# Scan stage of a two-layer hybrid mixer: one state step, one scaling and one set of turns moved in the instruction order

## The reference

```python
# latent attention: 4 heads, keys = 128 context + 1024 latent tokens
p = softmax(q @ k.T * scale);  o_mla = p @ v
# GLA, both directions, chunks of 64: gates, scores inside the chunk, state between chunks
q_dec, k_inv = q * exp(g), k * exp(-g)
o = tril(q_dec @ k_inv.T) @ v + q_dec @ s;   s = s * decay + k_end.T @ v
# gated DeltaNet, both directions, chunks of 64, 8 heads
m = strict_tril(k_beta @ k.T * decay)
t_inv = inverse(I + m)                        # triangular, unit diagonal
u, w = t_inv @ (v * beta), t_inv @ (k_beta * exp(g))
v_new = u - w @ s;  o = q_dec @ s + a @ v_new;  s = s * exp(g_last) + k_end.T @ v_new
```

## Time and profile before

| | |
|---|---|
| median of 3 runs | 4552.74 us (4550.39 to 4554.0) |
| profiled execution | 4550.52 us, of which the span is 4548.7 us |
| granted TensorE clock, mean | 0.925 of full speed |
| TensorE matmul / weight load | busy 3934.8 us (87%) / 3081.2 us (68%) |
| VectorE | busy 2176.4 us (48%) |
| ScalarE | busy 970.0 us (21%) |
| GpSimd | busy 1047.1 us (23%) |

### The profile page before, as it was taken

One profiled execution on the slowest core, in us unless ns is written; L12 is line 12 of the kernel. 1 busy time (PEld: TensorE's weight loads), 2 busy tenths in 40 slices (PEclk: granted clock), 3 DMA queues, 4 the chain that ended last, 5 costly groups with the idle time before them and its releaser, 6 DMA issues. The chain is left out here.

```text
span 4548.7 us, 81512 instructions
## 1 busy us (share of the span) xinstructions
PE 3934.8 (87%) x34010; PEld 3081.2 (68%) x34010; DVE 2176.4 (48%) x4932; ACT 970.0 (21%) x1898; POOL 1047.1 (23%) x1092
## 2 busy tenths in 40 slices
PE   4999968888687999999779997788859599999994
PEld 3444546776347999999744444566645399999994
DVE  3335046565455445444453331566646544454444
ACT  1333134444110000000033322444421000000001
POOL 0036034553210000011040440445512101100003
PEclk8999978888888999999989998898879799999997
DMA  7556353331518999999674653243233299999995
GB/s 256 172 192 236 126 126 77 77 73 36 189 63 248 275 278 269 279 278 270 183 233 147 240 192 87 70 99 81 63 117 121 105 271 269 275 278 276 271 279 179
DMA packets 822555, 836.27 MB, mean 184 GB/s; under 512 B 91976, under 2 KB 667528, under 8 KB 816044
## 3 DMA queue, kind: packets, MB, share of 16 engines
q1 hardware_dynamic: 740716, 711.23, 52.3%
q10 hardware_dynamic: 69856, 80.89, 5.3%
q0 software_dynamic: 11616, 38.94, 3.8%
HBM read 698.83 MB, written 132.10 MB: 183 GB/s over the span
## 5 line engine op out<-in xcount | busy, mean ns | idle before, releaser
L2500 PE MATMUL ffn_hb<-ffn_xT,ffn_w 128*128 128x144 f32 x8192 | 1057.4, 288 | 12.9 <-DVE ffn_xT L2613 6.5
L2500 PEld LDWEIGHTS ffn_hb<-ffn_xT,ffn_w 128*128 128x128 f32 x8192 | 1027.9, 191 | 15.7 <-DMA ffn_w<-in_w_e 6.9
L509 PE MATMUL front_acc<-front_w,front_xmT 128*128 128x512 f32 (+2 forms) x2304 | 881.8, 542 | 19.7 <-DVE front_xmT L768 17.4
L509 PEld LDWEIGHTS front_acc<-front_w,front_xmT 128*128 128x128 f32 x2304 | 439.1, 193 | 449.0 <-issue 419.3
L2508 PE MATMUL ffn_acc<-ffn_hT,ffn_w 128*128 128x144 f32 x4096 | 548.5, 287 | 0.0
L2508 PEld LDWEIGHTS ffn_acc<-ffn_hT,ffn_w 128*128 128x128 f32 x4096 | 519.7, 190 | 0.8
L2548 ACT ACTIVATE ffn_en<-ffn_hb 128x144 f32<-128x144 f32 x256 | 74.3, 290 | 1483.7 <-PE ffn_hb L2500 1483.7
L2432 POOL DMA_INDIRECT ffn_xe<-scratch_xhat,ffn_g_idx x34 | 34.5, 1014 | 1376.5 <-DVEq L2602 1376.5
L2647 DVE TENSOR_TENSOR ffn_hT<-ffn_en,ffn_hb 128x144 f32<-128x144 f32 x256 | 77.7, 303 | 529.8 <-ACT ffn_en L2548 528.9
L2224 PE MATMUL mixer_acc<-mixer_wout,mixer_oT 128*128 128x512 f32 x576 | 254.0, 599 | 0.0
L2571 DVE TENSOR_SCALAR_CACHE_REDUCE ffn_junk<-ffn_row,ffn_pair 128x128 f32<-128x128 f32 (+2 forms) x324 | 245.6, 758 | 6.3 <-DVE ffn_yp L2620 4.9
(11 more groups left out here) (322 smaller groups left out, 5195.0 us busy)
## 6 DMA issues: line engine op xcount, KB each, us to landing
ffn_w<-in_w_e SPq DMA_DIRECT2D x768, 512.0 KB, 6.4
x_res<-in_w_mod SPq DMA_DIRECT2D x40, 1024.0 KB, 5.4
x_res<-scratch_proj SPq DMA_DIRECT2D x36, 768.0 KB, 6.1
scratch_proj<-front_out ACTq DMA_DIRECT2D x90, 256.0 KB, 2.2
ffn_row<-scratch_affT SPq DMA_DIRECT2D x36, 576.0 KB, 6.3
front_w<-in_w_in ACTq DMA_DIRECT2D x8, 2048.0 KB, 12.5
scan_qk<-scratch_qkv SPq DMA_DIRECT2D x16, 1024.0 KB, 10.0
scratch_qkv<-x_res SPq DMA_DIRECT2D x18, 768.0 KB, 3.5
```

The lines of the kernel that those rows point to most:

```text
L509: mm = pe.matmul(acc[:, U % 2, 0:size], xmT[:, k, t * P:(t + 1) * P], w[:, n % 2, k, 0:size], start=k == 0, stop=k == KD - 1)
L2500: mm = pe.matmul(hb[:, b, i * CAP:(i + 1) * CAP], w[:, r, k, :], xT[:, s, k, :], start=k == 0, stop=k == KD - 1)
```

## The change

Nothing is added and nothing removed; instructions are placed elsewhere in the engines' programs. L numbers below are those of the kernel before.

```diff
--- before.py
+++ after.py
@@ -1501,32 +1501,32 @@
                     if g > 1:
                         gla_gates(g, h)
                         attend(at + 1)
-                        read_state(k, 2)
                         attend(at + 2)
                         gla_turn(g, h)
+                        attend(at + 3)
+                        gla_scores(g, h)
+                        read_state(k, 2)
+                        gla_values(g, h)
+                        attend(at + 4)
+                        gla_state(g, h, 0)
                         write_state(k, 2)
+                        attend(at + 5)
+                        gla_state(g, h, 1)
+                        read_state(k, 3)
+                        h = halves[g][1]
+                        attend(at + 6)
+                        gla_gates(g, h)
+                        write_state(k, 3)
+                        attend(at + 7)
+                        gla_turn(g, h)
+                        attend(at + 8)
                         gla_scores(g, h)
-                        attend(at + 3)
+                        attend(at + 9)
                         gla_values(g, h)
-                        read_state(k, 3)
+                        attend(at + 10)
                         gla_state(g, h, 0)
-                        attend(at + 4)
+                        attend(at + 11)
                         gla_state(g, h, 1)
-                        write_state(k, 3)
-                        h = halves[g][1]
-                        attend(at + 5)
-                        gla_gates(g, h)
-                        attend(at + 6)
-                        gla_turn(g, h)
-                        attend(at + 7)
-                        gla_scores(g, h)
-                        attend(at + 8)
-                        gla_values(g, h)
-                        attend(at + 9)
-                        gla_state(g, h, 0)
-                        attend(at + 10)
-                        gla_state(g, h, 1)
-                        attend(at + 11)
                     for i in range(n):
                         merge_x(g, i)
                     for i in range(n):
@@ -1734,17 +1734,17 @@
                         gla_turned(h)
                         attend(at + 3)
                         gla_values(h)
-                        attend(at + 4)
-                        attend(at + 5)
+                        for i in range(4, 7):
+                            attend(at + i)
                         h = halves[g][1]
                         gla_gates(h)
-                        attend(at + 6)
+                        attend(at + 7)
                         gla_turned(h)
-                        attend(at + 7)
                         attend(at + 8)
+                        attend(at + 9)
                         gla_values(h)
-                        for i in range(9, 12):
-                            attend(at + i)
+                        attend(at + 10)
+                        attend(at + 11)
                     for i in range(n):
                         merged_x(g, i)
                     for i in range(n):
@@ -1990,11 +1990,13 @@
                             first_latents(j)
                         for m in range(2):
                             masked_grams(g, m)
-                        for j in range(4):
+                        first_latents(6)
+                        for j in range(3):
                             block_in(g, (j,))
-                            first_latents(6 + j)
+                            first_latents(7 + j)
+                        block_in(g, (3,))
+                        gla_scaled(h)
                         block_scaled()
-                        gla_scaled(h)
                         attend(at)
                         gla_masked(h)
                         attend(at + 1)
@@ -2002,29 +2004,31 @@
                         gla_state(h, 0)
                         attend(at + 3)
                         gla_state(h, 1)
-                        for i in range(at + 4, at + 12):
+                        for i in range(at + 4, at + 10):
                             attend(i)
                         inverse_for_x(g)
+                        attend(at + 11)
                         inverse(1, ta_v)
                         inverse(2, ta_v)
-                        attend(at + 12)
-                        attend(at + 13)
                         inverse(0, tb_v)
                         inverse(3, tb_v)
+                        attend(at + 13)
                     else:
                         read_state(k, 0)
                         write_state(k, 0)
                         read_state(k, 1)
                         for m in range(2):
                             masked_grams(g, m)
-                        write_state(k, 1)
+                        if g == 1:
+                            write_state(k, 1)
                         for m in range(2, chunks[g]):
                             masked_grams(g, m)
                         block_in(g, (0, 1))
                         attend(at + (g == 1))
-                        block_in(g, (2, 3))
+                        block_in(g, (2,))
+                        gla_scaled(h)
+                        block_in(g, (3,))
                         block_scaled()
-                        gla_scaled(h)
                     if g == 1:
                         attend(at + 3)
                         gla_masked(h)
@@ -2038,29 +2042,31 @@
                         gla_masked(h)
                         attend(at + 11)
                     if g > 1:
+                        write_state(k, 1)
+                        gla_masked(h)
+                        attend(at + 2)
                         read_state(k, 2)
-                        attend(at + 2)
+                        gla_state(h, 0)
                         write_state(k, 2)
-                        gla_masked(h)
-                        read_state(k, 3)
-                        gla_state(h, 0)
                         attend(at + 4)
                         gla_state(h, 1)
+                        read_state(k, 3)
+                        h = halves[g][1]
+                        attend(at + 6)
+                        gla_scaled(h)
                         write_state(k, 3)
-                        h = halves[g][1]
-                        gla_scaled(h)
-                        attend(at + 6)
+                        attend(at + 8)
                         gla_masked(h)
-                        attend(at + 8)
+                        gla_state(h, 0)
                     if g:
                         inverse_for_x(g)
-                        gla_state(h, 0)
-                        inverse(1, ta_v)
+                        if g == 1:
+                            gla_state(h, 0)
+                            inverse(1, ta_v)
+                        gla_state(h, 1)
                         if g > 1:
-                            inverse(2, ta_v)
-                        gla_state(h, 1)
-                        if g == 1:
-                            inverse(2, ta_v)
+                            inverse(1, ta_v)
+                        inverse(2, ta_v)
                         inverse(0, tb_v)
                         inverse(3, tb_v)
                         attend(at + (13 if g == 1 else 10))
```

## The result

The changed kernel is slower: 4567.37 us (median of 7 runs, 4558.86 to 4570.61) against 4550.44 us (7 runs, 4544.78 to 4554.0), ratio 1.003 with a 95% interval of 1.002 to 1.004. The forecast was 4524.8 us.

A forecast was written before the change was run, and what follows sets the result against it. Bound: a chain through several engines in the scans. Per scan -5.0 (group 0), +0.6 (group 1), -3.75 (group 2), -5.8 (groups 3 and 4) is -13.95; two scans -27.9 take 4552.74 to 4524.8 us, range 4512 to 4541.

The forecast's parts named there:

- the one on the GLA loads: SyncE's loads behind the later state store: landing 5.2 us after issue, at 950.2, ahead of TensorE's need at about 953.
- first sign of being wrong: Stated test of failure: TensorE waits over 1 us for scan_E loads at the second piece.
- the second: Stated test of failure: L1859 starts over 3 us behind the substitution's end in groups 3 and 4.
- The slower rival: Late GLA loads at 12.5 us meet a TensorE keeping nothing of the 4.30 us, in six groups: 4568 us; chance 6%.
- five bits of slack: Argument against the slower case: this much slack would have to go at once for L1859 to be that late.
- The scores step: TensorE, second piece: one more such step ahead of the first update's matmuls makes L1859 1.05 us later in groups 3 and 4.
- D - L1851: Time from L1851 to the start of L1859 in a group; that start was forecast +1.05 us in groups 3 and 4.
- nothing of the 4.30 is kept: Upper bound for L1859 in groups 3 and 4 if TensorE's saved wait for the scaling is lost: +3.5 us.
- GpSimd's second instruction: In the substitution: without the scaling beside it, the first two instructions take 0.25 us; substitution 0.6 us shorter.
- From group 0's L1851 to group 1's: Group 0: L1859 directly at the substitution's end and weights sooner, 5.0 us gained a scan, bounds 4.0 and 5.5.
- Its wait for state step 1: New TensorE wait, since that state step now comes behind L1851: about 1.1 us.
- The sum of 27.9: Total gain in us forecast for the two scans, 13.95 in each.

The follow-up runs named there:

- e1_store_late: Changed kernel with SyncE's store of state step 1 moved behind the loads of gates, queries and keys in groups 2 to 4; 4531.43 us, ratio 0.9965 to before.
- e9_gla_first: Changed kernel with SyncE's GLA load ahead of the loads of gates, queries and keys, the store still first; 4529.92 us, ratio 0.9963 to before.
- e4_step1_back: Changed kernel with VectorE's state step 1 back between the masks, ahead of the substitution; 4526.37 us, ratio 0.9954 to before.
- e11_half_load: Changed kernel without the query loads of groups 3 and 4, old queries used instead; 4543.78 us, ratio 0.9997 to before.
- e13_tail_alone: Kernel before with only the new order behind the substitution's begin in groups 2 to 4; 4552.61 us, ratio 1.0013.
- e12_first_and_sooner: Changed kernel with the GLA load ahead of gates, queries and keys, and the second piece's first update ahead of a scores step on TensorE; 4525.59 us, ratio 0.9953.
- e2_before_held: Kernel before, with SyncE alone waiting for the substitution's begin ahead of storing state step 1 in groups 2 to 4; 4554.9 us, ratio 1.0018.

## Why the prediction was wrong

**The step that failed** is the one on the GLA loads: "With the usual 5.2 us to landing they are there at 950.2, ahead of TensorE's need at about 953. The queries and keys are in flight at the same time." The issue was forecast well: the last of the four in group 3 starts at 945.36 (I had them end near 945.0). The landing was not: 14.6 us instead of 5.2. The second sentence held the answer, and I gave it no price in the sum: TensorE's wait for this load stands there at nothing. Two loads of 1024 KB are 2.1 MB, at the 210 GB/s that the windows show 10 us of full DMA engines, and 10 + 4.8 is about the 14.6 measured. The usual 5.2 was, in all groups, that of loads sent 22 us or more behind the queries and keys. The trace of before had the other case too, at the start of the scan, where GLA's loads go out right behind group 0's queries and keys and a load of 1024 KB into x_res (DMA view of 577 to 584 us):

```profile
scan_qk<-scratch_qkv SPq DMA_DIRECT2D x2, 512.0 KB, 7.1
x_res<-scratch_proj SPq DMA_DIRECT2D x1, 1024.0 KB, 10.9
scan_E<-scratch_gla_la SPq DMA_DIRECT2D x2, 128.0 KB, 12.0
```

The second of these two scan_E loads took 12.5 us: it is the maximum of the earlier trace rows, which I used as a bound without asking what had made it so long. e1_store_late, e9_gla_first and e4_step1_back each take the queries and keys from ahead of the GLA load and get the time back; e11_half_load gets it back by half. In profiles: L1859 was to start 39.8 and 40.6 us behind L1851 in groups 2 and 3; it came 8.4 and 10.3 later, and 8.1 and 10.3 in the second scan, 37 us together. The two scans were to shrink by 27.9 and grew by 15.3. Of these 43 us e9_gla_first and e1_store_late, which repair the load alone, get back 34.9 and 37.6. The prediction's first sign of being wrong (over 1 us of wait for scan_E) came true with 7.52 us, the second (L1859 over 3 us behind the substitution's end) in group 3 with 11.2; in group 4 it was 2.9.

The Trainium skill (DMA: Bandwidth & Descriptors, Queues, rings and completion order) says that one issuing engine has one ring on each DMA engine and that its descriptors are consumed in ring order. The trace agrees: 14.6 us behind 2 MB, 5.2 ahead of them. The order in the ring is not the whole of it, since ScalarE's 64 KB load took 11.1 us in the same stretch and 3.0 without it.

**The slower rival** named this mechanism and gave 4568 us, but its number fits by chance. It had six groups at 12.5 us; there were four at 14.4 to 14.9, for group 4 has no queries and keys ahead of its load. I gave it 6%, because "five bits of slack would have to go at once". They did not have to: the wait on the load alone, 7.52 and 6.33 us, was longer than the 4.7 us from which I had said that this case decides.

**The scores step** was seen and half right. With the load repaired, VectorE is late at L1859 in groups 3 and 4: D - L1851 of 40.5 and 40.2 in e9_gla_first, 42.5 and 41.3 in e1_store_late, where I had 40.6 (second scan: 40.5 and 42.5, 42.5 and 42.3). Why e1_store_late is later than e9_gla_first in group 3 is open. The bound "nothing of the 4.30 is kept", 3.5 us later, is what e13_tail_alone shows (3.4 to 6.0 later in the first scan, 2.0 to 5.8 in the second). e12_first_and_sooner takes the scores step away and the lateness goes.

**Terms that held.** merge_x starts at 884.42, D + 5.33, and weights at 892.82, D + 13.73 (forecast 5.3 and 13.6; before D + 10.8 and D + 17.55):

```profile
884.42 3.63 PE L1207 MATMUL scan_pA<-scan_NB,scan_PM 32*32 32x32 f32 x128 [3.79 <-DVE scan_SG L1909]
...
892.82 1.99 PE L1233 MATMUL scan_pA<-scan_TT,scan_Rk 64*64 64x64 f32 x64 [0.64 <-ACT scan_TT L1582]
```

The number of `weights` held, its reason only in part: the profile has it released by ScalarE's copy of merge_z (L1582), which I had at D + 12.8. The last quadrant ends 0.25 us before weights starts, so both end together.

GpSimd's second instruction takes 0.24 us, where it took 0.57:

```profile
831.64 0.24 POOL L1787 TENSOR_TENSOR scan_Tb<-scan_Tb,scan_prod 128x30 f32<-128x30 f32 x1
```

From group 0's L1851 to group 1's it is 3.4 and 5.0 us less in the two scans (forecast 5.0). TensorE's wait ahead of L1375 is gone in groups 1 to 4; in group 0 2.87 us of it are left (3.60 before). Its wait for state step 1 is 2.25 us in group 3, where I had 1.1, and 3.71 in group 4.

**The sum of 27.9** was too large even with the load repaired: with every step of the engines where the change put it, the two scans are 19.6 us shorter (e9_gla_first) and 22.3 (e1_store_late), the medians by 0.37 and 0.35% where the forecast had 0.6. Only a further edit comes near it: 26.7 us with state step 1 back (e4_step1_back), 25.3 with the update ahead of the scores step (e12_first_and_sooner). Nor do the parts add. Alone, group 0 gives 0.12%, the scaling costs 0.09% and the tail costs 0.13%, together a loss of 0.1%; in e4_step1_back they gain 0.46%. Each of these has an interval of about 0.1% to either side, far less than the difference. The tail needs either the earlier scaling or the update ahead of the scores step.

## What to carry to other kernels

When a step moves, look at the in-order queue that stores its result and price every transfer behind it: bytes over the bandwidth of the full DMA engines, for each load that now comes directly ahead of a needed one. A median time to landing says little about a load with a full queue ahead, and the maximum in the same row may be just that case: look at what stood ahead of it. And an order that adds slack on one engine (the scaling) may be worth nothing alone and decide another edit, so such parts are to be timed in pairs.

## What the runs showed of the hardware

TensorE can stop with nothing to wait for that the profile shows, while the DMA engines are full; a late refill of its instructions is the likely reason, not a shown one. The four stops of 3.3 to 4.4 us in e2_before_held each fall together with one instruction packet and a DMA share of about 1; with 1 MB less in the queue two of them fell to 2.7 and 2.6 us and two below 1. The changed kernel has one as well, of 3.12 us in group 3 of the second scan, and e11_half_load one of 2.54 us there and one of 1.76 in group 2 of the first. e9_gla_first had the same 16 us of full engines and no stop over 1.4 us apart from the one of about 2 us in group 0 that every kernel here has, before included, so full engines alone do not make one; which matmuls stand there may matter too, and what exactly decides is open. The Trainium skill (Runtime: NRT & Kernel Launch, Instruction fetch mechanics) calls the cost of crossing into the next block of instructions mostly hidden; if these stops are such crossings, up to 4.44 us was not hidden here.

Full DMA engines delayed another engine's queue too, not only the one with the large loads: ScalarE's load of 64 KB took 11.1 us beside SyncE's 2 MB and 3.0 without them.

A wait costs more than its length: TensorE's granted clock fell during the 7.52 us (0.56 from 850 to 854) and was 0.50 behind them until about 862, the lower of its two levels, and its matmuls there took 1.7 to 1.9 times as long as in group 4 (2.08 against 1.08 us, 1.71 against 0.95).
